# Last three feed-forward chunks computed for two token groups, then streamed again for the third group

## The reference

```python
h = x * (1 + mod[:, 1]) + mod[:, 0]
x = layer_norm(ALPHA * x + 0.5 * mod[:, 2] * swiglu(h, ffn1_wg, ffn1_wu, ffn1_wd), ln_g[0], ln_b[0])
h = x * (1 + mod[:, 4]) + mod[:, 3]
out, k_a, v_a, k_b, v_b = mixer(l, h)          # one projection w_in, attention, w_out
x = layer_norm(ALPHA * x + mod[:, 5] * out, ln_g[1], ln_b[1])
h = x * (1 + mod[:, 7]) + mod[:, 6]
x = layer_norm(ALPHA * x + 0.5 * mod[:, 8] * swiglu(h, ffn2_wg, ffn2_wu, ffn2_wd), ln_g[2], ln_b[2])
```

## Time and profile before

| what | value |
|---|---|
| median of 3 runs | 2372.83 us |
| profiled execution, own time | 2374.0 us |
| its span, first to last instruction | 2372.1 us |
| TensorE (PE) busy | 2214.4 us, 93% |
| VectorE, ScalarE, GpSimd busy | 782.0, 542.7, 701.0 us |
| mean granted TensorE clock | 0.968 of full |
| DMA | 171.21 MB, mean 72 GB/s |

### The profile page before, as it was taken

The page is one execution under the profiler, slowest core; times in us unless marked ns, Lnnn a source line. Parts: engine busy times, 40 slices in busy tenths (PEclk is TensorE's granted clock), DMA queues, the critical chain, the costliest instruction groups (busy, mean ns, idle before and its releaser), DMA issues.

```text
span 2372.1 us, 33586 instructions
## 1 busy us (share of the span) xinstructions
PE 2214.4 (93%) x13352; PEld 2018.2 (85%) x13352; DVE 782.0 (33%) x1730; ACT 542.7 (23%) x956; POOL 701.0 (30%) x421
## 2 busy tenths in 40 slices
PE   6899999999999996999799879789999999999996
PEld 2799999999999985998644459579999999999994
DVE  2322311222212249012546521582222222222225
ACT  3111111111111112222345530321111121111114
POOL 2622232322232214234233352343232232332300
PEclk8899999999999997999899989989999999999998
DMA  7463221322311000422521011201111111111001
GB/s 275 148 198 107 90 82 61 97 99 91 105 40 51 27 18 9 159 72 72 179 102 72 1 36 40 76 19 42 47 53 35 53 48 40 53 37 51 27 1 72
DMA packets 167763, 171.21 MB, mean 72 GB/s; under 512 B 14234, under 2 KB 130698, under 8 KB 167156
## 3 DMA queue, kind: packets, MB, share of 16 engines
q1 hardware_dynamic: 167668, 169.84, 22.1%
HBM read 156.91 MB, written 19.20 MB: 74 GB/s over the span
## 4 chain that ended last, share of the span: by engine, by line
PE 84%; DVE 7%; ACT 2%; POOL 2%; SPq 2%; issue 2%; DMA 1%; DVEq 0%; POOLq 0%; ACTq 0%
PE psum L211 24%; PE psum L213 24%; PE psum L212 24%; PE psum L1018 2%; PE psum L495 2%; PE psum L567 1%; PE psum L1077 1%; PE psum L919 1%; DVE NT L631 1%; DVE Y L592 1%; POOL Hlo L724 1%; PE psum L1367 1%; DMA ADA<-in_w_ada 1%; SPq L448 1%; DVE RSTD L607 1%
## 5 line engine op out<-in xcount | busy, mean ns | idle before, releaser
L211 PE MATMUL psum<-Hhi,Whi 128*128 128x344 f32 x2736 | 883.8, 323 | 59.8 <-POOL Hlo L724 30.4
L213 PE MATMUL psum<-Hhi,Wlo 128*128 128x344 f32 x2736 | 879.2, 321 | 0.0
L212 PE MATMUL psum<-Hlo,Whi 128*128 128x344 f32 x2736 | 878.9, 321 | 0.0
L211 PEld LDWEIGHTS psum<-Hhi,Whi 128*128 128x128 f32 x2736 | 519.7, 190 | 70.1 <-issue 53.8
L311 POOL TENSOR_TENSOR Wlo<-RAW,Whi 128x1024 fp32r<-128x1024 f32 x158 | 383.4, 2446 | 632.2 <-ACT Whi L307 631.6
L213 PEld LDWEIGHTS psum<-Hhi,Wlo 128*128 128x128 f32 x2736 | 519.4, 190 | 0.0
L212 PEld LDWEIGHTS psum<-Hlo,Whi 128*128 128x128 f32 x2736 | 519.0, 190 | 0.2
L400 DVE TENSOR_TENSOR GF<-SIL,psum 128x344 f32<-128x344 f32 x132 | 67.7, 513 | 910.8 <-ACT SIL L382 910.8
L418 DVE SCALAR_TENSOR_TENSOR Y<-psum,G,Y 128x344 f32<-128x344 f32 (+1 forms) x528 | 302.5, 573 | 190.6 <-PE psum L213 190.5
L211 PE MATMUL psum<-Ghi,Whi 128*128 128x344 f32 x1056 | 339.6, 322 | 3.3 <-DVE yS L421 1.7
L212 PE MATMUL psum<-Glo,Whi 128*128 128x344 f32 x1056 | 338.0, 320 | 0.0
(11 more groups left out here) (189 smaller groups left out, 1396.5 us busy)
## 6 DMA issues: line engine op xcount, KB each, us to landing
ADA<-in_w_ada SPq DMA_DIRECT2D x38, 1024.0 KB, 9.2
RAW<-in_ffn_wg SPq DMA_DIRECT2D x44, 512.0 KB, 3.8
RAW<-in_ffn_wu SPq DMA_DIRECT2D x44, 512.0 KB, 3.7
RAW<-in_ffn_wd SPq DMA_DIRECT2D x44, 512.0 KB, 3.5
RAW<-in_w_in SPq DMA_DIRECT2D x36, 256.0 KB, 3.2
SK<-in_cache_a_k SPq DMA_DIRECT2D x24, 256.0 KB, 3.4
SK<-in_cache_a_v SPq DMA_DIRECT2D x24, 256.0 KB, 3.7
joint_rows<-joint_heads SPq DMA_DIRECT2D x1, 4608.0 KB, 28.0
```

The lines of the kernel that those rows point to most:

```text
L211: pe.matmul(out, whi, xhi, start=first, stop=False)
L212: pe.matmul(out, whi, xlo, start=False, stop=False)
L213: return pe.matmul(out, wlo, xhi, start=False, stop=last)
```

## The change

The last three chunks of each feed-forward (8, 9, 10) are computed for groups 0 and 1 only, as three runs of four up units and 16 down products. Then the same three chunks are streamed from memory a second time and computed for group 2 alone, as three runs of two up units and 8 down products. PIECES goes from 66 to 84 for each feed-forward. The statistics of groups 0 and 1 are placed between the units of the second streaming, and all means and variances of norms 1 and 3 use PSUM bank 7, so that a mean waits for the std of the group before it. The projection begins with its first four tiles for groups 0 and 1, then for group 2; weight slots 2 and 3 serve tiles 2 and 3. The output's first transposes stand ahead of the mean and variance of group 2. The diff cut to its core:

```diff
-        PIECES = {"ffn1": 6 * CH, "proj": PT, "wout": KT, "ffn2": 6 * CH}
+        PIECES = {"ffn1": 6 * (CH + 3), "proj": PT, "wout": KT, "ffn2": 6 * (CH + 3)}
-        MEAN_BANK, VAR_BANK = (0, 1, 2), (7, 6, 5)
+        MEAN_BANK, VAR_BANK = {1: (7, 7, 7), 2: (0, 1, 2), 3: (7, 7, 7)}, {1: (7, 7, 7), 2: (7, 6, 5), 3: (7, 7, 7)}
...
+        FIRST_TWO = [(0, 0), (0, 1), (1, 0), (1, 1)]
...
+        LC = 3
+        LF = CH - LC
...
+        def tail_pe(pe, x, n, ada=()):
+            for r in range(LF, CH):
+                ub, db = two_groups_at(r)
+                ffn_pe(pe, x, r, ub, db, FIRST_TWO, ada if r == LF else (), down0=db % 3)
+            def up(r, j):
+                if r < CH + LC:
+                    pe.wait_ge(x.w.ready, 6 * r + 3 + 2 * (j + 1))
+                    up_pe(pe, x, r, last_group_at(r)[0] + j, j, NG - 1, j)
+            pe.wait_ge(x.y_evac, last_group_at(CH)[1] - KT + 3)
+            mean_pe(pe, n, 0)
+            up(CH, 0)
+            var_pe(pe, n, 0)
+            up(CH, 1)
+            pe.wait_ge(x.y_evac, last_group_at(CH)[1] + 3)
+            mean_pe(pe, n, 1)
+            up(CH + 1, 0)
+            var_pe(pe, n, 1)
+            for r in range(CH, CH + LC):
+                ub, db = last_group_at(r)
+                pe.wait_ge(x.w.ready, 6 * r + 3 + 6)
+                pe.wait_ge(x.g_ready, ub + 4)
+                for d in range(KT):
+                    down_pe(pe, x, db + d, d, NG - 1, bank[4 + (db + d) % 3])
+                up(r + 1, 1)
+                up(r + 2, 0)
+        def tail_act(act, x, n):
...
+            for r in range(CH, CH + LC):
+                ub, db = last_group_at(r)
+                more = r + 1 < CH + LC
+                if r == CH:
+                    silu_act(act, x, ub, 0)
+                else:
+                    for s in (4, 5):
+                        ffn_split_hi(act, x, r, s, 0, db)
+                g_hi_act(act, x, ub, 0, 0, NG - 1, db)
+                if more:
+                    for s in (0, 1):
+                        ffn_split_hi(act, x, r + 1, s, ub + 1, 0)
+                elif n.mod:
+                    for q in (0, 1):
+                        split_hi(act, "proj", q, q, 0)
+                if r == CH:
+                    std(act, n, 0)
+                silu_act(act, x, ub + 1, 1)
+                g_hi_act(act, x, ub + 1, 1, 1, NG - 1, db)
+                if more:
+                    for s in (2, 3):
+                        ffn_split_hi(act, x, r + 1, s, ub + 2, 0)
+                if r < CH + 2:
+                    input_hi(act, n, r - CH, 0)
+                    input_hi(act, n, r - CH, 1)
+                if r == CH:
+                    square(act, n, 1)
+                if more:
+                    silu_act(act, x, ub + 2, 0)
+                if r == CH:
+                    std(act, n, 1)
+        def tail_dve(dve, x, n, ada=(), prepare=None):
...
+            center(dve, n, 0)
+            prepare()
+            for r in range(CH, CH + LC):
+                ub, db = last_group_at(r)
+                if r == CH:
+                    gf_dve(dve, x, ub, 0)
+                    scaled(dve, n, 0, lambda: gf_dve(dve, x, ub + 1, 1))
+                    center(dve, n, 1)
+                elif r == CH + 1:
+                    scaled(dve, n, 1, lambda: gf_dve(dve, x, ub + 1, 1))
+                else:
+                    gf_dve(dve, x, ub + 1, 1)
+                if r + 1 < CH + LC:
+                    gf_dve(dve, x, ub + 2, 0)
+                for d in range(KT):
+                    down_dve(dve, x, db + d, d, NG - 1, bank[4 + (db + d) % 3])
+        def tail_pool(pool, x, n):
...
+            for r in range(CH, CH + LC):
+                ub = last_group_at(r)[0]
+                more = r + 1 < CH + LC
+                if r > CH:
+                    for s in (4, 5):
+                        ffn_split_lo(pool, x, r, s)
+                g_lo_pool(pool, x, ub, 0, 0, NG - 1)
+                if more:
+                    for s in (0, 1):
+                        ffn_split_lo(pool, x, r + 1, s)
+                elif n.mod:
+                    for q in (0, 1):
+                        split_lo(pool, "proj", q, q, q)
+                g_lo_pool(pool, x, ub + 1, 1, 1, NG - 1)
+                if more:
+                    for s in (2, 3):
+                        ffn_split_lo(pool, x, r + 1, s)
+                if n.mod and r < CH + 2:
+                    input_lo(pool, n, r - CH)
...
+        def proj_first_pe(pe):
+            v = 0
+            for groups in (range(NG - 1), range(NG - 1, NG)):
+                for t in range(4):
+                    for g in groups:
...
+                        if v == 1:
+                            pe.wait_ge(resid_done, 1)
+                            mean_pe(pe, ln[1], NG - 1)
+                        if v == 3:
+                            var_pe(pe, ln[1], NG - 1)
...
             for b in range(TB + 1):
+                if b == 1:
+                    pe.wait_ge(resid_done, 3)
+                    mean_pe(pe, ln[3], 2)
+                if b == 3:
+                    var_pe(pe, ln[3], 2)
```

More of the change, by code:

```diff
@@ L334, in ffn_split_hi @@
[L334 to L341, removed]
-            for j in range(2):
-                if j and len(ada) == 2:
-                    ada_pe(pe, *ada[0])
[L345 to L357, removed]
+                act.wait_ge(x.down_done, free_down + UNIT_D)
@@ new lines, in down_pe, with ffn_pe @@
+        def down_pe(pe, x, v, d, g, bk):
+            pe.wait_ge(x.y_evac, v + 1)
+            for j in range(2):
+                last = mm3(pe, bk[:, 0:TG], Whi[4 + j][:, d, :], Wlo[4 + j][:, d, :],
+                           Ghi[j][:, group(g)], Glo[j][:, group(g)], j == 0, j == 1)
+            last.then_inc(x.down_done, 1)
+        def ffn_pe(pe, x, r, ub, db, units, ada=(), norm=None, down0=0):
+            for i, (j, g) in enumerate(units):
+                if i == 3 and len(ada) == 2:
+                    ada_pe(pe, *ada[0])
+                if g == 0:
+                    pe.wait_ge(x.w.ready, 6 * r + 3 + 2 * (j + 1))
+                up_pe(pe, x, r, ub + i, j, g, i)
@@ L358, in ffn_pe @@
             if ada:
                 ada_pe(pe, *ada[-1])
-            pe.wait_ge(x.w.ready, 6 * c + 3 + 6)
-            for g in range(NG):
-                pe.wait_ge(x.g_ready, 6 * c + g + 6)
+            pe.wait_ge(x.w.ready, 6 * r + 3 + 6)
+            for g in range(len(units) // 2):
+                pe.wait_ge(x.g_ready, ub + units.index((1, g)) + 3)
                 for d in range(KT):
                     v = KT * g + d
[L365 to L370, removed]
+                    down_pe(pe, x, db + v, d, g, bank[4 + (down0 + v) % 3])
@@ L376, in ffn_pe @@
                     mean_pe(pe, norm, g - 1)
[L378 to L401, removed]
+        def silu_act(act, x, u, i):
+            act.wait_ge(x.up_done, u + 7)
+            act.wait_ge(x.gf_done, u + 1)
+            act.activation(SIL[i % 2][:, :], bank[2 * (i % 2)][:, 0:TG], ACT.Silu).then_inc(x.silu_done, 1)
@@ L402, in ffn_dve @@
+        def ffn_dve(dve, x, r, ub, db, units, ada=(), before=None, norm=None, down0=0, done=0):
+            for i in range(done, len(units)):
+                if before is not None and (not done and i < NG):
+                    norm_y(dve, before, i)
+                gf_dve(dve, x, ub + i, i)
+                if before is not None and done:
+                    norm_y(dve, before, i - done)
             turns = ada and ada[-1][2]
@@ L1777, in _ @@
             dve.sem_inc(resid_done, 1)
-            prep(dve, None, None, 2, last_norm=True)
-            norm_dve(dve, ln[3])
-            for b in range(2, TB + 1):
+            out_half(dve, 0, 0)
+            center(dve, ln[3], 2)
+            for b in range(1, 3):
+                out_half(dve, b, 0)
+            scaled(dve, ln[3], 2)
+            for b in range(3, TB + 1):
                 out_half(dve, b, 0)
```

278 lines of the change are left out of this document (187 added, 91 removed).

## The result

| | before | changed |
|---|---|---|
| median of five executions each | 2373.0 us | 2386.39 us (2381.95 to 2388.51) |
| ratio, 95% interval | | 1.0050 [1.0038, 1.0062] |
| profiled execution, its own time | 2374.0 us | 2381.95 us, the lowest of the five |
| its span | 2372.1 us | 2380.2 us |

The change costs 0.5%, some 11.8 us [9.0, 14.7]. That is slower, by the bound of 0.2% that the prediction set itself. It lies inside the forecast's range (2362 to 2387), yet the likeliest case, +3.8 us and within 0.2%, is not what came. The profiled execution shows +8.1 us of span. The readings that follow explain those 8.1; the rest lies between executions, and the first experiment comes back to it.

What follows compares the result with a forecast made beforehand. PE, busy 93% of the span, was taken as the bound, so only its waits and slow stretches could change. Norm 1 -3.7 and norm 3 +7.5 gave +3.8 us, 2376.6 from a median of 2372.83; range 2362 to 2387.

Steps and rivals of the forecast that it cites:

- the likeliest case: Whole kernel: norm 1 gains 3.7 us, norm 3 loses 7.5, sum +3.8 us, 2376.6; chance 0.40.
- a worse projection fetch: Norm 1, last down products: stall of 11 us instead of 9.3 if four transfers share the queue badly.
- norm 1: down(CH+2): Last down products of feed-forward 1: Glo stands behind the projection tiles' fetch and splits, 9.3 us of stall.
- norm 1: projection start: Group 2's Hlo is ready on POOL at 40.1 where PE wants it at 39.5; costed at 0.7 us.
- the 29.5 and 62.5 of the kernel before: Before the change: 29.5 us lost at norm 1; 62.5 us at norm 3's end, including group 0's mean and a 0.8 wait.
- norm 3: down(CH+2): Last down products of feed-forward 2: silu, GF, Ghi and Glo stand bare with hand-overs, 2.9 us of stall.
- norm 3: from the last down product to the end: Output: block 0, group 2's mean and variance, scaling, identities and remaining blocks take 37.0 us, 34.5 at full clock.
- First stall, up(CH+2,0): Third single-group run: late weights cost 4.4 us, POOL waiting for DVE's series adds more; 10.8 at norm 1, 8.3 at norm 3.
- the light rival: POOL slips between DVE's instructions, so first stalls are 4.4 us in both norms; sum -7.5, 2365.3; chance 0.27.
- Nothing waits until here: Single-group runs up to up(CH+1,1), ending at 56.3 us: PE has no wait; group 1's square ready at 34.7, wanted at 36.6.
- The clock falls twice: Second slow stretch behind each of four stalls and the wait before the last variance, 5 x 1.5 us; sum +11.3, 2384.1; chance 0.31.
- for a square: Sign of failure: the prediction is wrong if PE waits earlier than up(CH+2,0), for a square or a std.

Runs made afterwards that it cites:

- the first experiment: Changed kernel unedited, 1.0061 against the kernel before; only feed-forward 1 and projection start changed, 1.0021; only feed-forward 2 and output changed, 1.002.
- the kernel with small Wlo: Changed kernel with POOL computing only an eighth of each Wlo in the single-group runs, fetches and matmuls kept: 2354.57 us, 0.9923 against the kernel before.
- the reordered kernel: Changed kernel with CH+2 slots 0, 1 before CH+1 slots 4, 5, group 1's `center` earlier, last Glo before projection splits: 0.9943, run again 0.9924.
- the two-chunk kernel: Changed kernel with two chunks streamed twice instead of three, plus `center` of group 1 earlier and last Glo before the projection's splits: 2362.53 us, 0.9955.

## Why the prediction held in its range and failed in its mechanism

The measured 2386.39 us lies 0.6 us below the upper end of the range, and it is there by luck: that end was set by a second fall of the clock and a worse projection fetch, and neither came. The schedule was right in shape and mostly in size, norm 3 well and norm 1 not. In the profiled execution, worked out as in the prediction:

| term, us | predicted | measured |
|---|---|---|
| norm 1: up(CH+2,0) | 10.8 | 5.1 |
| norm 1: down(CH+2) | 9.3 | 8.9 |
| norm 1: slow stretches behind these two | 5.0 | 4.2 |
| norm 1: projection start | 0.7 | 1.1 |
| norm 1: variance, wait and slow stretch | 0 | 7.4 |
| norm 1: in down(CH+1), wait and slow stretch | 0 | 4.1 |
| norm 1, all, from the first single-group mean to the fourth projection tile | 25.8 | 31.5 |
| norm 3: up(CH+2,0) | 8.3 | 5.1 |
| norm 3: down(CH+2) | 2.9 | 2.7 |
| norm 3: slow stretches behind these two | 3.2 | 3.7 |
| norm 3: from the last down product to the end | 37.0 | 37.7 |
| norm 3, all | 70.0 | 68.2 |

A slow stretch is the time from the end of a wait to the next one less 0.157 us a matmul. The measured totals are differences of times on PE's timeline, so norm 1 holds 0.7 us and norm 3, with the four statistics at 18.6, 0.4 us that no row names. Against the 29.5 and 62.5 of the kernel before, norm 1 gives +2.0 and norm 3 +5.7, together +7.7 of the span's +8.1.

**The step that failed** is the contention of POOL and DVE in "First stall, up(CH+2,0)": "so it waited for the whole series. I take that: +4.0". From one Glo of 4.09 us, which came into a series under way, I took POOL to be the one that waits. That row was the exception: the Glo at the same place of the program took 1.15 or 1.16 us in each of the twelve other profiles, as the first Glo of the earlier trace rows did (1.16). In the changed kernel POOL has a queue of splits (its first runs from 50.0 in the prediction's own schedule, DVE's series starts at 52), and it is DVE that waits, one POOL instruction for each of its own. So the 4.0 and 2.5 us were put on the wrong engine. The stalls for Wlo were 5.08 in both norms, near the 4.4 of the queue alone. The additions had no part in them: they begin at 870.11, when the stall is over. The eight scalar_tensor_tensor had a small one: the four splits and the Glo of rows 856.54 to 862.74 took about 1 us more than at their usual length (11.5 against 10.6). Freed from contention the forecast would have been the light rival's, 2365.3, and further off.

**What the same mistake hid** is "Nothing waits until here". It used 2.55 us for the additions of group 0, so that the square of group 1 was ready 1.9 us before PE wanted it. They took 10.45 us beside POOL's splits and Hlo, and the square came 4.75 us late. Doing `center` first gained the 7 us back, which shows the cause. The wait of 2.67 us inside down(CH+1) has the same source: the additions of group 1 (10.47 us) keep DVE from emptying the PSUM bank. It fell to 2.27 us in that kernel, where these additions were still 10.46 us long, and was gone in the kernel with small Wlo (additions 3.65 us) and in the one with only the order of the pieces changed (2.55 us).

The Trainium skill (SBUF — State Buffer, Who interferes with whom) says that whichever of the two engines starts first holds the shared port for the whole of its instruction, and that issue order decides who blocks. The trace agrees on DVE's side: one DVE instruction for each split, 2.6 us each. On POOL's side the traces show both: 1.05 us and 2.58 us for a Glo that came 0.74 us into the same kind of series, so there the order of issue did not decide. I had weighed this rule for POOL's wait alone and never asked what it would do to DVE; the page also names `tensor_scalar`, the additions, among the operations that can enter the modes that take the shared port.

**Right**: the two stalls in each norm and their releasers, the price of Glo's place behind the projection's fetch and splits (8.9 against 9.3, and 7.4 us came back when it moved), the 11 us wait that goes, the slow stretches of 1.9 to 2.6 us behind each long wait (behind the wait of 2.71 us it was 1.6, not 0.7), and the output's end within 0.7 us. That the bytes cost nothing by themselves was right as far as the runs show: with all of them fetched, the reordered kernel has no wait for a landing or a split in its single-group runs.

**The rivals.** "The clock falls twice" had the right sign but not the mechanism: each wait of the single-group runs has one slow stretch behind it and no second; the loss was two waits that I had at zero, with the stretches behind them. Light contention held for POOL and failed for DVE. The prediction named the sign of its own failure, a wait "for a square". The 0.35 that I gave to slower came mostly from that rival, so it stood on the wrong mechanism. It was also too low by its own working: with its spread of 4 us, read as one standard deviation, some 0.16 of the forecast's 0.40 lies beyond +4.7, and with the rival's 0.31 that is 0.47.

**Open**: about 4 us between the profiled execution and the medians, the two groups of the kernel in the new order, and what decides whether POOL or DVE waits when a single Glo comes into a series: Glo that came 0.74 us into the additions waited for the series in four of eighteen cases. No run varied the moment of arrival by itself.

## What to carry to other kernels

When a stage is cut to half its matmuls, write down each helper engine's work per microsecond of matmul again, and set the order of its queue by what PE wants next, not by index: moving two pieces, one `center` and one pair of splits turned 1.0050 into 0.9943 and, run again, 0.9924. Contention between VectorE and GpSimd must be costed for both sides: ask what each would lose, and what waits for it. One row of a trace is not enough to say who loses. A chain that is bare at the end of a run (activation, product, rounding, remainder) has to be followed through all three engines, as the two-chunk kernel showed when DVE's series turned up ahead of it.

## What the runs showed of the hardware

- A VectorE series beside GpSimd's back-to-back splits ran at one instruction per split: eight scalar_tensor_tensor in 11.48 us instead of 3.99, eight tensor_scalar in 10.45 instead of 2.55, within 0.03 us in every kernel whose queue of splits was the same. The splits went from 2.42 to 2.6 us. With splits an eighth as wide the same series took 4.54 and 3.65 us. A single GpSimd instruction that came 0.7 us into a VectorE series waited for all of it in some cases (4.09 us for 0.93 before the change; 2.58 to 2.61 for 0.91 in four profiles of the kernels with moved pieces or with two chunks and the other edits) and for next to nothing in others, at the same distance and in the same kind of series (1.05 and 1.16 us in the changed kernel), where one VectorE instruction waited instead.
- An add of one SBUF tensor and a per-partition scalar is hit like an operation with two SBUF tensors: 10.45 us for 2.55.
- In the single-group runs each TensorE wait of 4.75 us and more was followed by matmuls at half clock, with a mean granted clock of 0.62 to 0.79 over the 13 to 16 us around three of them. A wait of 2.71 us mostly was too, with a delay: at norm 3 the matmuls ran for 0.8 us at 0.32 us each, then 11 took 0.49, which makes 1.6 us. In the kernel with all three reorderings the same wait at norm 1 was followed by 11 such matmuls in one profile and by none in the other.
